# A mixture-of-experts trunk on one core: one 128-row block per pass, weights streamed anew for further blocks

## What is computed

```python
logits = (ht @ w_router + b_router).astype(jnp.float32)
top_val, top_idx = lax.top_k(logits, TOP_K)          # 4 of 32 experts per token
top_w = jax.nn.softmax(top_val, axis=-1)
...
def expert_block(args):                              # xb: 128 token rows of one expert
    xb, e = args
    gu = xb @ w_gate_up[e] + b_gate_up[e]            # 1024 x 2048 weights
    return clamped_swiglu(gu) @ w_down[e] + b_down[e]    # 1024 x 1024 weights
...
out = jnp.zeros((t + 1, d), ys.dtype).at[row_tok].add(ys)[:t]
```

## Time and profile before

| | us |
|---|---|
| median of 3 runs | 1947.07 (1945.6 to 1949.34) |
| the profiled execution, its own time | 1943.69 |
| its span, first to last instruction | 1941.2 |
| first expert matmul starts | 526.77 |
| last expert matmul starts | 1880.10 |

### The profile page before, as it was taken

How to read it: one execution, slowest core, us unless ns; L and a number is a source line. 1 busy time by engine, 2 the same in 40 slices (tenths; PEclk the granted TensorE clock), 3 DMA queues, 4 the chain that set the end, 5 groups by cost and what they waited for, 6 DMA issues and landing times.

```text
span 1941.2 us, 24261 instructions
## 1 busy us (share of the span) xinstructions
PE 1693.3 (87%) x7526; PEld 1305.4 (67%) x7527; DVE 1315.4 (68%) x1024; ACT 1027.8 (53%) x922; POOL 249.1 (13%) x232
## 2 busy tenths in 40 slices
PE   6999986686389999999899999999989999999860
PEld 1788854443277787778787778877878777788640
DVE  0454458734378888576788788856678878676645
ACT  2322234431266777465677677745567676465530
POOL 2000000012301111011111111201111111011110
PEclk9899986788599999999999999999999999999885
DMA  7676440011589999677899999977789999777735
GB/s 232 201 243 209 156 122 1 4 58 65 198 302 335 344 372 363 208 277 273 309 362 351 327 345 363 364 266 248 272 319 366 346 331 336 247 270 283 270 125 219
DMA packets 245634, 499.09 MB, mean 257 GB/s; under 512 B 16796, under 2 KB 17928, under 8 KB 244738
## 3 DMA queue, kind: packets, MB, share of 16 engines
q1 hardware_dynamic: 228288, 458.26, 66.4%
q0 software_dynamic: 14448, 34.73, 5.2%
q10 hardware_dynamic: 2610, 2.11, 0.3%
HBM read 490.23 MB, written 27.09 MB: 266 GB/s over the span
## 4 chain that ended last, share of the span: by engine, by line
PE 65%; DMA 5%; issue 5%; DVE 2%; POOL 2%; ACT 1%; POOLq 1%; ACTq 0%; DVEq 0%
PE ps L1048 18%; PE ps L1050 18%; PE ps L1049 18%; PE ps L993 3%; PE ps L622 3%; PE ps L1054 2%; DMA xy<-h_ffn,icur 2%; DMA expert_rows<-xy,icur 1%; DMA x1e<-x_after_mixing 1%; POOL icur L1353 1%; PE ps L642 0%; POOL icur L1334 0%; DVE yo L1410 0%; ACT wh L1163 0%; PE ps L424 0%
## 5 line engine op out<-in xcount | busy, mean ns | idle before, releaser
L1240 DVE TENSOR_TENSOR wl<-rawm,wh 128x2048 fp32r<-128x2048 f32 x384 | 875.4, 2289 | 287.9 <-ACT wh L1163 282.7
L1163 ACT ACTIVATE wh<-rawm 128x2048 fp32r<-128x2048 f32 x384 | 736.3, 1918 | 450.9 <-PE ps L1050 446.0
L1048 PE MATMUL ps<-wh,xh 128*128 128x512 f32 x1120 | 468.1, 418 | 7.6 <-issue 5.3
L1050 PE MATMUL ps<-wh,xl 128*128 128x512 f32 x1120 | 440.4, 393 | 0.2 <-issue 0.2
L1049 PE MATMUL ps<-wl,xh 128*128 128x512 f32 x1120 | 440.0, 393 | 0.0
L1048 PEld LDWEIGHTS ps<-wh,xh 128*128 128x128 f32 x1120 | 214.4, 191 | 49.1 <-issue 6.2
L1050 PEld LDWEIGHTS ps<-wh,xl 128*128 128x128 f32 x1120 | 212.5, 190 | 47.8 <-issue 1.3
L1049 PEld LDWEIGHTS ps<-wl,xh 128*128 128x128 f32 x1120 | 213.3, 190 | 43.2
L1048 PE MATMUL ps<-wh,ah 128*128 128x512 f32 x560 | 239.3, 427 | 3.4 <-issue 3.4
L1050 PE MATMUL ps<-wh,al 128*128 128x512 f32 x560 | 221.4, 395 | 0.0
L1049 PE MATMUL ps<-wl,ah 128*128 128x512 f32 x560 | 221.3, 395 | 0.0
(11 more groups left out here) (224 smaller groups left out, 1690.5 us busy)
## 6 DMA issues: line engine op xcount, KB each, us to landing
rawm<-in_w_gate_up SPq DMA_DIRECT2D x256, 1024.0 KB, 6.5
rawm<-in_w_down SPq DMA_DIRECT2D x128, 1024.0 KB, 6.4
raw<-in_w_ada SPq DMA_DIRECT2D x24, 1024.0 KB, 16.3
raw<-in_w_in SPq DMA_DIRECT2D x16, 1024.0 KB, 5.5
yt<-expert_rows POOLq DMA_DIRECT2D x4, 2048.0 KB, 9.1
wo<-in_w_out SPq DMA_DIRECT2D x2, 2048.0 KB, 16.9
bias_vectors_repeated<-bias_vectors POOLq DMA_DIRECT2D x1, 2304.0 KB, 16.5
xs<-in_x ACTq DMA_DIRECT2D x1, 2048.0 KB, 24.7
```

Source lines behind the costliest of these rows:

```text
L1048: nc.tensor.matmul(dst, a_h[:, b, kk, :], wh[:, place.split(v), k, :], start=False, stop=False)
L1050: ins = nc.tensor.matmul(dst, a_l[:, b, kk, :], wh[:, place.split(v), k, :], start=False, stop=kk == KC - 1)
L1163: nc.scalar.activation(flat(wh[:, place.split(v), :, :]), flat(rawm[:, place.slot(v), :, :]), ACT.Copy).then_inc(wh_done, 1)
L1240: nc.vector.tensor_tensor(flat(wl[:, place.slot(v), :, :]), flat(rawm[:, place.slot(v), :, :]), flat(wh[:, place.split(v), :, :]), ALU.sub ...
```

## The change

- One block per pass, always. The loop runs over the 32 experts' first blocks without any test; the further blocks come at the end as passes of their own, up to 15, each of which streams its expert's 12 MB again. VectorE works out beforehand which expert and which column of the table each of them takes (`plan_dve`); only these last passes test a register.
- A half is now 256 rows by 1024 columns, 4 KB a row, 1 MB as before. There are 12 slots, one for each half of a pass. A half still serves 12 matmuls, now alternating between two PSUM banks, with each stationary piece used twice in a row.
- Up comes before gate. The activation steps work on 1024 columns at once rather than 512.
- Tokens are gathered into `xb`, outputs leave from `yb`; a gather no longer waits for a scatter.
- The slot table holds (token, row) pairs, so `gtab` and its shift go; the four clears of `xy` become one clear of `xb`, issued earlier.
- The first halves are loaded earlier, and ScalarE and VectorE split the first four before they treat the first tokens.
- Loop iterations have five passes (`TURN = 5`); passes 0 and 1 stand before the loop.

```diff
-RAW, SPL = 8, 4
-TURN = 6
+HALVES, SPL = 12, 4
+TURN = 5
+MORE = 15
...
+    rows = np.stack([rows // TOPK, rows], 2)
...
-    slot_d = dram("slot_rows", (T * E, 1), I32)
+    slot_d = dram("slot_rows", (T * E, 2), I32)
...
+            if t == TC - 1:
+                sp.wait_ge(ya_ps, TC)
+                load_half(sp, 2, gate_up_half(0, 2))
+                sp.wait_ge(yb_ps, TC)
+                load_half(sp, 3, gate_up_half(0, 3))
...
+    def gate_up_half(e, v):
+        k, col = v % 4, FF if v < UP else 0
+        return w_gate_up[0, bass.ds(e, 1), 2 * k * P:2 * (k + 1) * P, col:col + FF].rearrange("a (k p) n -> p (a k) n", p=P)
...
+    def first_passes(eng, body):
+
+        body(0, 0, None)
+        body(1, 1, 0)
+        with nc.Fori(0, (E - 2) // TURN, engines=[eng.engine], hint_back_edge=True) as k:
+            for i in range(TURN):
+                p = k * TURN + (2 + i)
+                body(p, p, p - 1)
...
+    def further_passes(eng, count, body, j=0, d=E - 1):
+
+        if j == MORE:
+            return
+        with eng.If(count >= j + 1):
+            e = planned_expert(eng, E + j)
+            body(E + j, e, d)
+            further_passes(eng, count, body, j + 1, e)
...
+        def multiplied(banks, p, v, slot, a_h, a_l):
+
+            pe.wait_ge(wl_done, used(p, v))
+            for k in range(2):
+                kk = 2 * (v % 4) + k
+                for left, right in ((a_h, wh[slot % SPL]), (a_h, wl[slot]), (a_l, wh[slot % SPL])):
+                    for n in range(2):
+                        ins = nc.tensor.matmul(banks[:, n, :], left[:, kk, :], right[:, k, n * UN:(n + 1) * UN],
+                                               start=False, stop=kk == KC - 1 and left is a_l)
+            ins.then_inc(half_used, 1)
+
+        def body(p, e, d):
+            pe.wait_ge(xl_done, p + 1)
+            if not is_first(p):
+                pe.wait_ge(u_ready, p)
+            biased(UPPED, e, D)
+            for v in range(UP):
+                multiplied(UPPED, p, v, v, xh, xl)
+            if not is_first(p):
+                pe.wait_ge(g_ready, p)
+            biased(GATED, e, 0)
+            for v in range(UP, N_GU):
+                multiplied(GATED, p, v, v, xh, xl)
+            tokens_transposed(p + 1)
+            if is_first(p):
+                acts_transposed(p)
+                pe.wait_ge(nk_ready, 1)
+                return
+            if not (isinstance(p, int) and p == 1):
+                pe.wait_ge(y_copied, p - 1)
+            biased(DOWNED, d, 2 * D)
+            for v in range(DOWN, HALVES):
+                if v == HALVES - 1:
+                    acts_transposed(p)
+                multiplied(DOWNED, p, v, v, ah, al)
...
+        def gather(p, table_column):
+            if not is_first(p):
+                pool.wait_ge(xt_done, p)
+            column(0, p + 1, table_column, gcur)
+            pool.indirect_dma_start(out=xb[:], out_offset=None, in_=h2_d,
+                                    in_offset=bass.IndirectOffsetOnAxis(ap=icur[:, 0:1], axis=0),
+                                    bounds_check=T - 1, oob_is_err=False).then_inc(xg_in, 16)
```

More of the change, by code:

```diff
@@ L845, in program @@
     half_used, wh_done, wl_done = map(sem, ("half_used", "wh_done", "wl_done"))
[L846 to L849, removed]
+    rawm_in = raw_in + [sem(f"rawm_in{s}") for s in range(4, HALVES)]
+    xg_in, xt_done, xh_done, xl_done, gcur, scur = map(sem, ("xg_in", "xt_done", "xh_done", "xl_done", "gcur", "scur"))
@@ L968, in experts_sync @@
             sp.wait_ge(h2_out[w], 32)
-        def load(place, v, src, free=True):
-            if free:
-                sp.wait_ge(half_used, place.count(v) - RAW)
-            sp.dma_start(rawm[:, place.slot(v), :, :], src).then_inc(rawm_in[place.slot(v)], 16)
-        def body(e, place, has_d):
-            for v in range(N_GU):
-                if not has_d and v == 6:
-                    sp.wait_ge(lg_ps, TC)
-                load(place, v, gate_up_half(e, v), free=has_d)
-            if has_d:
-                for d in range(N_D):
-                    load(place, N_GU + d, down_half(e - 1, d))
@@ L1039, in further_acts_split @@
-        def further_acts_split(x):
-            with pe.If(x.more >= 1):
-                x.prefix()
-                pe.wait_ge(al_done[1], x.all_more(1, 0))
-                pe.sem_inc(passed, 1)
-        def multiply(dst, place, v, b, h, a_h, a_l):
-            for k in range(HK):
-                kk = HK * h + k
-                nc.tensor.matmul(dst, a_h[:, b, kk, :], wh[:, place.split(v), k, :], start=False, stop=False)
-                nc.tensor.matmul(dst, a_h[:, b, kk, :], wl[:, place.slot(v), k, :], start=False, stop=False)
-                ins = nc.tensor.matmul(dst, a_l[:, b, kk, :], wh[:, place.split(v), k, :], start=False, stop=kk == KC - 1)
-            return ins
@@ L1361, in experts_pool @@
-        first = Expert(pool, 0)
-        gather(first, None)
-        def body(e, gathers=True):
-            if not (isinstance(e, int) and e < 2):
-                scatter(Expert(pool, e - 2))
-            if gathers:
-                gather(Expert(pool, e + 1), None if isinstance(e, int) and e == 0 else Expert(pool, e - 1))
-        body(0)
-        body(1)
-        with nc.Fori(2, E - 1, engines=[pool.engine], hint_back_edge=True) as e:
-            body(e)
-        body(E - 1, gathers=False)
@@ L1375, in experts_pool, with body @@
-        scatter(Expert(pool, E - 2))
-        scatter(Expert(pool, E - 1))
+        for p in range(3):
+            gather(p, p + 1)
+        with nc.Fori(3, E, engines=[pool.engine], hint_back_edge=True) as p:
+            scatter(p - 3, p - 2)
+            gather(p, p + 1)
+        count = further_blocks(pool)
+        scatter(E - 3, E - 2)
+        gather(E, planned_column(pool, E))
+        def body(p, e, d):
+            scatter(p - 2, planned_column(pool, p - 2))
+            gather(p + 1, planned_column(pool, p + 1))
@@ L1379, in program @@
+        further_passes(pool, count, body)
+        for p in (count + (E - 2), count + (E - 1)):
+            scatter(p, planned_column(pool, p))
+        return count
     fin_out = [sem("fin_out0"), sem("fin_out1")]
```

661 lines of the change are left out of this document (245 added, 416 removed).

## The result

The changed kernel has a median of 1859.12 us (1856.96 to 1860.75, 4 runs), the kernel before in the same session 1946.34 us (1944.03 to 1949.34, 4 runs). The ratio is 0.955 [0.9533, 0.9567]: 4.5% faster, some 87 us. The forecast was 1887 us, 60 less, with a range down to 1868. Its sign and most of its mechanism hold; its size does not.

The account below looks back on a forecast made before the run. TensorE's clean block pace bounds the kernel: 35 x 35.98 = 1259.3 us, plus 2.4, 9.4, 11.6, 5.9 and 7.9, is 1296.5. With start and end 60.5 us less: 1887 us; own range 1868 to 1905, 8 in 10 1868 to 1922.

Parts of the forecast that it names:

- Clean pace: Expert stage: 35 blocks at 35.98 us each, the pass in which nothing waits, 1259.3 us.
- Back edges and exit: Expert loop on TensorE: five back edges cost 11.6 us, the exit into the further passes 5.9 us.
- Low clock at the start, fill and tail: Expert stage: first matmuls at low clock 2.4 us; fill 9.4 and tail 7.9 us, waits for activations included.
- The start: Before the first expert matmul: shift, register load and test go, 1.5 us; weights split ahead, 2.3 us; 3.8 saved.
- The end: After the last expert matmul: the last output is one copy instead of two halves, 0.5 us more.
- forecast of 1296.5: Expert stage: clean passes plus start clock, fill, back edges, exit and tail, 1296.5 us against 1353.7 before.
- The 94.4: Expert stage before: 1353.7 us against 1259.3 at clean pace; 94.4 us lost, all the change can win there.
- 61.1 us of waits: TensorE's waits in the old stage: issue 31.6, token gather 18.5, first low parts 5.5, last activations 5.5 us.
- the issue waits stay: Rival, expert loop: code is fetched as late without the tests, the other 20.7 us remain, 1915 us; chance 0.12.
- VectorE: Rival: VectorE, 91% busy, holds up TensorE each pass; 1922 us at 1 us a pass; chance 0.08.
- The transfers: Rival: DMA of the loop's weights bounds; slower than before below 343 GB/s; chance 0.10, 0.07 below that point.
- The further blocks: Three further passes with 12 MB each: 37.7 MB more traffic, 364 GB/s without a break, costed at 0.

Follow-up runs that it names:

- the first kernel with the edit of fill and tail: Changed kernel with pass 1's tokens transposed during pass 0, pass 0's activations transposed inside pass 1, activations split before the next weights: 1846.23 us, 0.9495.

## Why the gain was larger than predicted

The prediction counted a clean pace for all blocks, and what remained on top. The profiled executions went from 1943.69 to 1860.75, 82.9 us less, where 60.5 were forecast. Term by term:

- **Clean pace**: predicted 35.98 a pass, measured 35.84. Over 35 passes 4.9 us better. A pair of biases with 48 matmuls between them takes 11.36 us, against 2 x 5.70. The two forms also differ in which bank follows which and in `x2` of each stationary piece; no run parts them. The two biases, in the timeline of TensorE after:

```profile
1061.77 0.61 PE L1005 MATMUL ps<-bparts,sel 96*128 96x512 bf16 x2
...
1073.13 0.61 PE L1005 MATMUL ps<-bparts,sel 96*128 96x512 bf16 x2
```

- **Back edges and exit**, 11.6 + 5.9 = 17.5: measured 0. This is the step that failed: "What stays are the loop's back edges." I read four issue waits, each at a back edge, and took the edge for the cause. But of the 19 issue waits in the stage before, 14 stood neither at a back edge nor at the exit, among them one of 3.8 us at 1082.18. The cause was what lay behind it: a turn that did not stay resident, with code to be jumped over. Runs with 3 and with 15 turns have the same time.
- **Low clock at the start, fill and tail**, 2.4 + 9.4 + 7.9 = 19.7: measured 18.3, from 1272.7 for the stage less 35 x 35.84. The sizes were right.
- **The start**: 3.8 predicted, 0.6 measured. "The shift, the register load and the test in between go" held, and so did the weights split ahead: from bias to first matmul 2.4 us were won. Of the 3.2 that are missing, 2.2 lie between the last four slot scatters and the table's read, where two of them are slow, which the prediction did not have; 0.6 is that the scatters started later in this trace (498.00 against 497.39), and 0.4 that the table's read took 6.3 us from issue to use against 5.9 (506.96 to 512.82 before). The step did not ask what shares the stretch from the scatters to the gather: the splits and loads that were moved ahead now run beside it. Of the loads only the 0.4 can be seen against before, where the read was nearly as slow; holding back the `down` loads wins 3.5 us beyond that.
- **The end**: 0.5 us more predicted, 0.6 less measured (60.7 to 60.1 from the end of the last matmul to the end of the span), and 0.6 less outside the span.

The stage alone thus came 23.8 us below its forecast of 1296.5, the start 3.2 above, the rest 1.7 below: 22.3, against 82.9 - 60.5 = 22.4. The remaining 5 us or so of the median's distance of 28 lie in how the two profiled executions stand to their medians: 3.4 below before, 1.6 above after.

The loss that the change took back is split by the chain of runs, by the ratios: the never-run code of blocks 2 and 3, 40 us; a turn short enough to stay resident, 17; the gather's own tile, 21; all the rest of the change (pace, straight code, wide pieces, start and end), 10. By the 95% intervals each step has an uncertainty of 6 to 8 us. In the stage alone, one trace each, the steps are 37.7, 20.2, 14.8 and 8.2 us. The 94.4 was not passed: the fastest stage, 1261.7 us in the first kernel with the edit of fill and tail, is 92.0 below that of before. The prediction also named both causes. It counted 61.1 us of waits where the stage has 66.0, since the earlier trace rows lacks a line, and it could not tell that the code cost 57 us: its rows show 31.6.

The rivals: **"the issue waits stay"** fell, with no issue wait at all. **VectorE** did not become the bound: it is busy for 793 of 900 us and TensorE never waits for it in the loop. **The transfers** did not, with 8% more traffic either. The further blocks did cost nothing, as the prediction had it.

## What to carry to other kernels

A loop on TensorE can pay for code that it only jumps over, while straight code was free here even when fetched anew. Drop branches that cannot be taken, or keep a turn under the size that stays resident, and count the packets on the instruction queue to see which of the two you have. Give a gather a tile of its own, so that neither an output nor a landing stands before it. Test how much room a transfer has with one more megabyte per pass, before you count on or fear a share near 1.0.

## What the hardware did that I had not expected

- Fetching straight code again, at 53 and 54 packets in the stage, cost nothing measurable (0.9547 and 0.9549 against 0.955), and neither did back edges. With forward jumps over unused code in the turn, 191 packets went with 36 us of issue waits; without that code and with a turn that fits, these were 5.3, and the low clock in the stage cost 15 us less.
- The DMA share says nothing of headroom here: 0.99 at 365 GB/s, 1.02 at 395 GB/s, both without a wait.
- A small read with some megabytes of weights under way took 6.0 to 6.4 us from issue to use in eight traces, against 2.8 and 2.9 in the two in which the last four loads were held back.
- Two slot scatters took GpSimd 2.5 and 1.9 us in place of 0.96 in every kernel in which VectorE splits weights at the same time. Whether that is the cause is open.
